# One 4 MB transfer in place of two for the gate/up weights of pairs 6 to 29

## What is computed

```
def swiglu(x, wg, wu, wd):
    return (jax.nn.silu(x @ wg) * (x @ wu)) @ wd
y = routed_experts(xf, top_idx, top_w, w_gate, w_up, w_down) + swiglu(xf, ws_gate, ws_up, ws_down)
```

## Time and profile before

| | |
|---|---|
| median of 3 runs | 1197.84 us |
| the profiled execution | 1197.3 us |
| its span, first to last instruction | 1195.5 us |
| TensorE busy | 1148.2 us (96%) |
| the queue of SyncE's transfers, share of 16 DMA engines | 91.0% |
| read from memory | 452.22 MB, 381 GB/s over the span |
| gate/up transfers of 2 MB | 128, of them 96 in pairs 6 to 29 |

### The profile page before, as it was taken

The page is one execution under the profiler, slowest core; times in us unless marked ns, Lnnn a source line. Parts: engine busy times, 40 slices in busy tenths (PEclk is TensorE's granted clock), DMA queues, the critical chain, the costliest instruction groups (busy, mean ns, idle before and its releaser), DMA issues.

```text
span 1195.5 us, 15901 instructions
## 1 busy us (share of the span) xinstructions
PE 1148.2 (96%) x6752; PEld 520.0 (43%) x6752; DVE 352.7 (29%) x1053; ACT 254.9 (21%) x509; POOL 8.4 (1%) x20
## 2 busy tenths in 40 slices
PE   7999999999999999999999999999999999999995
PEld 6774533433343333333386655433433343333331
DVE  0424622222222322222333346232223222222224
ACT  1132321222122111111112323221222122211110
POOL 0000000000000000000000000000000000000001
PEclk9999999999999999999999999999999999999998
DMA  9973699999999999999997626999999999999994
GB/s 386 422 319 112 232 365 423 427 428 426 427 428 428 427 428 427 427 426 428 420 419 320 256 83 238 398 429 427 425 428 427 428 428 427 428 425 426 428 429 201
DMA packets 36928, 456.49 MB, mean 382 GB/s; under 512 B 4080, under 2 KB 4208, under 8 KB 7024
## 3 DMA queue, kind: packets, MB, share of 16 engines
q1 hardware_dynamic: 36848, 455.38, 91.0%
HBM read 452.22 MB, written 3.15 MB: 381 GB/s over the span
## 4 chain that ended last, share of the span: by engine, by line
PE 72%; DMA 23%; DVE 3%; issue 1%; ACT 0%; POOL 0%; SPq 0%; POOLq 0%; DVEq 0%
PE bank L685 27%; DMA slots<-in_w_gu 20%; PE bank L724 13%; PE bank L874 5%; PE bank L802 5%; PE bank L586 4%; PE bank L613 4%; DMA slots<-in_dense 3%; PE bank L811 2%; PE bank L821 1%; PE bank L701 1%; PE bank L831 1%; PE bank L907 1%; PE bank L637 1%; PE bank L757 1%
## 5 line engine op out<-in xcount | busy, mean ns | idle before, releaser
L685 PE MATMUL bank<-slots,front 128*64 128x512 f32 x2048 | 456.1, 595 | 18.8 <-DMA slots<-in_w_gu 18.5
L685 PEld LDWEIGHTS bank<-slots,front 128*64 128x64 f32 x2048 | 138.0, 137 | 288.1 <-issue 251.6
L724 PE MATMUL bank<-slots,r 128*32 128x512 f32 x2016 | 233.0, 595 | 1.5 <-issue 1.1
L1332 DVE SCALAR_TENSOR_TENSOR yparts<-bank,small,yparts 128x512 fp32r<-128x512 f32 x128 | 96.0, 750 | 269.3 <-ACT yparts L1034 269.3
L1034 ACT ACTIVATE yparts<-bank,small 128x512 fp32r<-128x512 f32 x128 | 88.0, 687 | 245.3 <-PE bank L724 245.3
L1324 DVE TENSOR_TENSOR high<-high,bank 128x256 f32<-128x256 f32 x64 | 27.0, 421 | 357.3 <-ACT high L1061 357.3
L1061 ACT ACTIVATE high<-bank 128x256 f32<-128x256 f32 x64 | 24.6, 384 | 448.2 <-PE bank L685 448.2
L724 PEld LDWEIGHTS bank<-slots,r 128*32 128x32 f32 x2016 | 60.3, 109 | 134.8 <-issue 134.0
L1034 ACT ACTIVATE front<-bank 128x512 f32<-128x512 f32 (+1 forms) x160 | 84.3, 583 | 83.5 <-PE bank L586 15.5
L586 PEld LDWEIGHTS bank<-selr,xparts 128*128 128x128 f32 x512 | 64.2, 188 | 45.4 <-issue 45.4
L613 PE MATMUL bank<-yparts 64*128 64x512 f32 x512 | 79.3, 422 | 1.7 <-DVE yparts L1332 1.7
(11 more groups left out here) (126 smaller groups left out, 615.8 us busy)
## 6 DMA issues: line engine op xcount, KB each, us to landing
slots<-in_w_gu SPq DMA_DIRECT2D x128, 2048.0 KB, 28.8
slots<-in_w_dn SPq DMA_DIRECT2D x62, 2048.0 KB, 30.8
slots<-in_dense SPq DMA_DIRECT2D x30, 1024.0 KB, 14.3
slots<-in_first SPq DMA_DIRECT2D x4, 768.0 KB, 7.7
r<-in_pool_mat SPq DMA_DIRECT2D x2, 1024.0 KB, 23.7
sdn<-in_shared_dn SPq DMA_DIRECT2D x2, 1024.0 KB, 10.0
spill<-xs SPq DMA_DIRECT2D x2, 1024.0 KB, 4.4
xs<-in_w_dn SPq DMA_DIRECT2D x2, 1024.0 KB, 5.1
```

What stands on the lines that cost most here:

```text
L685: m = pe.matmul(H[64 * a:64 * a + 64, :], cells[:, cell(B, k, j), a, :], GU[g][:, a, :, k, :], start=k == 0, stop=k == KD - 1)
L724: m = pe.matmul(Y[half][r0:r0 + 32, :], hT[:, kc * P + 64 * a + 32 * t:kc * P + 64 * a + 32 * t + 32], wd[a][:, kc, half * 512:(half + 1) ...
L1332: dve.scalar_tensor_tensor(ysp[:, 1, half * 512:(half + 1) * 512], Y[half][:, :], wslot[:, b:b + 1], ysp[:, 0, half * 512:(half + 1) * 512 ...
```

## The change

For pairs 6 to 29 (`WHOLE`) SyncE no longer issues two halves. It waits until pair n-3 has used all of its gate/up weights and then issues one transfer of 4 MB, 32 KB a partition, which counts on `w_in[1][g]`. TensorE waits for that one transfer before the first gate/up matmul of the pair; the wait before k = 4 is still there and is then already met. Pairs 0 to 5, 30 and 31 keep their two halves, and the further rounds keep them for all pairs. Down weights, the order of the queue and all computation stay as they are.

```
+WHOLE = range(6, PAIRS - 2)
+HALVES = [[q for q in range(g, PAIRS, 3) if q not in WHOLE] for g in range(3)]
...
                 def body(n, q, g, b, use, first, last):
-                    sp.wait_ge(ps.h_half, n - 2)
-                    load_gu(ps, l, q, g, (0,))
-                    sp.wait_ge(ps.h_full, n - 2)
-                    load_gu(ps, l, q, g, (1,))
+                    if round_ is None and q in WHOLE:
+                        sp.wait_ge(ps.h_full, n - 2)
+                        sp.dma_start(slots[:, g, 0:2 * W_CHUNK], w_gu[l * PAIRS + q]).then_inc(ps.w_in[1][g], 16)
+                    else:
+                        sp.wait_ge(ps.h_half, n - 2)
+                        load_gu(ps, l, q, g, (0,))
+                        sp.wait_ge(ps.h_full, n - 2)
+                        load_gu(ps, l, q, g, (1,))
                     sp.wait_ge(ps.y_full, 2 * (n - 2))
...
-                    pe.wait_ge(ps.w_in[0][g], (turn * USES[g] + use) * 16 + 16)
+                    if round_ is not None:
+                        pe.wait_ge(ps.w_in[0][g], (turn * USES[g] + use) * 16 + 16)
+                    elif q not in WHOLE:
+                        pe.wait_ge(ps.w_in[0][g], (turn * len(HALVES[g]) + HALVES[g].index(q)) * 16 + 16)
+                    else:
+                        pe.wait_ge(ps.w_in[1][g], (turn * USES[g] + use) * 16 + 16)
```

## The result

The changed kernel takes 1201.39 us (median of 8 runs, 1199.33 to 1203.82), the kernel before 1198.15 us in the same comparison (8 runs, 1196.59 to 1198.83). The ratio is 1.0027 with a 95% interval of 1.0016 to 1.0038: slower by 3.2 us (1.9 to 4.6). The profiled execution has a span of 1199.8 us and 1201.64 us in all, against 1195.5 and 1197.3 before.

The account below looks back on a forecast made before the run. DMA was taken to bound most of each pass, TensorE its end. Lag less row gain, 2.84 − 1.3 + 3.51 − 1.4 = +3.6 us on 1197.84, gave 1201.4 us; 8-in-10 range 1198.7 to 1205.0.

Parts of the forecast that it names:

- What bounds the kernel: Passes over the experts: DMA is slower by 1.44 us a pair; after the last late weights TensorE alone sets the time.
- the sum: Both layers' lag less the row gain: 2.84 − 1.3 + 3.51 − 1.4 = +3.6 us, slower.
- The wait for the whole: Ends of both passes: TensorE starts late, 2.84 us remaining after layer 0 and 3.51 us in layer 1.
- The rows: Merged gate/up transfers: fewer, longer rows save 0.06 us a pair, 1.3 us in layer 0 and 1.4 in layer 1.
- The rival of pieces of 16 KB: 32 KB rows travel as two pieces, only the lag remains: +6.35, 1204.2 us; no gain from rows had chance 0.22.
- The rival of a larger gain: Longer rows pay more: from 0.088 us a merged pair the result is within 0.2%, at 0.14 nothing; chance 0.17.
- The later issue: First half's weights go out 3.4 us later; 3.9 us of queue at layer 1's pair 6 covers it: 0.
- Lag made up: Rival: pairs 28 to 31 at 13.24 us regain the lag, leaving 2.9 us saved: 1194.9 us; chance 0.07.
- Every transfer pays its start: Rival: each of 48 removed transfers saves a lone transfer's 2.3 us, 110 us in all: 1087 us; chance 0.01.

Follow-up runs that it names:

- the run with short rows: Pairs 6 to 24 as one 4 MB transfer each, but written in 16 KB rows, against the kernel before: 1199.31 us against 1199.18, ratio 1.0002.

## Why the prediction was right, point by point

- **What bounds the kernel.** Right: DMA paces the second part of a pass, and after the last late weights TensorE does. The end of the pass is where the change is paid. One reading was early: in the kernel before the first wait for a second half is that of pair 20 (0.40 us, at 418.60), not of pair 18 or 19; the sum doesn't use it.
- **The wait for the whole.** Right in place and size: 6.35 us in the sum, 7.1 us (5.4 to 8.7) by itself. 0.7 us of it vanish in the wait for layer 1's dense chunk, as worked out: the first matmuls of layer 1 come 2.6 us later than before, the line behind them 1.9. One detail differs: in layer 1 the last late weights were pair 27's, not pair 28's.
- **The rows.** Right in kind; the term of 0.06 us a merged pair measured 0.077 (43.82 against 44.05 us for three pairs; 0.07 between the medians of the longer stretch). The rival of pieces of 16 KB is ruled out by the packet count, and what it would have cost was seen in the run with short rows. The rival of a larger gain falls with 0.077, under the 0.088 that it needed, though not by much.
- **The later issue.** Wrong: taken as 0 because 3.9 us of queue covered it, it costs 1.7 us (0.6 to 2.8) by itself in the kernel with two transfers. Where it is lost is not shown, nor that the change pays as much: near pair 6, where the prediction looked for a gap, the change has none (DMA share 1.01 from 180 to 210 us and from 780 to 810), only 416 and 426 GB/s in place of 426 and 430 in these stretches. With this term the sum is 6.35 − 45 × 0.077 + 1.7 = 4.6 us, without it 2.9. The measured 3.2 (1.9 to 4.6) allows both. So that the forecast came out so near the measured time is in part luck: it holds two errors of opposite sign, a gain taken too small by 0.8 us and a cost left out.
- **Lag made up.** It did not happen in the change, for the reason given, and did as soon as `shared_down` was moved.
- **Every transfer pays its start.** Nothing of the 110 us appeared: one transfer in place of two with rows of the same length left the time where it was (ratio 1.0002, 0.9993 to 1.0011, with 38 transfers fewer). The Trainium skill's fixed cost of about 2.0 us per DMA (DMA: Bandwidth & Descriptors, "Anatomy of one DMA — SWDGE (gpsimd) path") is given there for the path of DMAs that GpSimd issues, and its rule to coalesce is for many small transfers. The queued 2 MB transfers of SyncE here don't pay such a cost one by one, by the same ratio.

## What to carry to other kernels

Joining two loads makes the consumer wait for the later of the two. While the loads are the bound, this wait is free; the lag is paid where the bound passes to the consumer, so look first at the end of the stage, and leave the loads split there early enough for the lag to be made up. What keeps the lag from being made up may be unrelated work: moving it is worth nothing alone and several microseconds together with the change.

## What the runs showed of the hardware

A packet of 32 KB in place of two of 16 KB saved 0.077 us in a transfer of 128 rows on 16 engines, 8 rows an engine: an estimated 10 ns a row. At 16 KB rows DMA ran at 427 to 428 GB/s, at two thirds of the bytes in 32 KB rows at 429 to 430.

Holding an issue back by 3.4 us in pairs 6 to 29 cost 1.7 us (0.6 to 2.8) although the transfers before it had at least 3.9 us to run and a lone transfer's start and completion take 2.3. Comparing these two numbers was not enough to call it free; which transfers lose the time is not shown. Held back from pair 3 on it cost 3.2 us, with DMA idle in between.

TensorE's granted clock fell to 0.50 inside a pass after single waits: for 6.8 us in and behind waits of 4.62 and 5.26 us (pairs 25 to 29 merged), for 3.4 us behind waits of 2.67 and 2.82 us (later issue). It did not fall inside a pass of the kernel before or of the changed one, where TensorE waits some 1.2 us in each pair, nor behind one wait of 2.66 us in the run with short rows.
